# Two of eight token tiles of a PEER layer computed over all experts on TensorE, six gathered, with the fronts of later tiles run ahead

## The reference, cut to what matters

```python
q = (h @ w_q).reshape(bsz, s, PEER_HEADS, 2, PEER_HALF)
scores = jnp.einsum('bshpd,pkd->bshpk', q, sub_keys)
s_top, i_top = lax.top_k(scores, PEER_TOPK)
...
expert = i1 * PEER_N_KEYS + i2          # 8 heads x 16 picks for each token
gates = jax.nn.softmax(best, axis=-1)
act = jnp.einsum('bthkd,btd->bthk', u[eb], xb)
w = gb * jax.nn.gelu(act, approximate=False)
out = jnp.einsum('bthk,bthkd->btd', w, v[eb])
```

## Time and profile before

| | |
|---|---|
| median of three runs | 4433.24 us |
| the profiled execution: its time | 4419.49 us |
| its span, first to last instruction | 4417.6 us |
| mean granted TensorE clock | 0.735 of full |
| DVE, POOL, PE busy | 53%, 54%, 55% |
| data moved | 1201.38 MB, mean 272 GB/s |

### The profile page before, as it was taken

The page is one execution under the profiler, slowest core; times in us unless marked ns, Lnnn a source line. Parts: engine busy times, 40 slices in busy tenths (PEclk is TensorE's granted clock), DMA queues, the critical chain, the costliest instruction groups (busy, mean ns, idle before and its releaser), DMA issues.

```text
span 4417.6 us, 33711 instructions
## 1 busy us (share of the span) xinstructions
PE 2446.3 (55%) x10844; PEld 1289.7 (29%) x10844; DVE 2342.8 (53%) x4908; ACT 891.9 (20%) x2805; POOL 2404.9 (54%) x2104
## 2 busy tenths in 40 slices
PE   8999878988881543532543453354345335423333
PEld 5778756565640121210120121012012001200000
DVE  3330077674008557557546655755665675575443
ACT  1310033232021211211211221121122112111111
POOL 1333100000006777777777767777777777777775
PEclk9999989999895766755765675576578557655555
DMA  2322242120507998999989999999999999999998
GB/s 84 128 95 86 85 149 69 43 72 29 201 34 260 351 340 326 362 363 352 359 330 363 352 351 363 350 362 359 365 347 359 363 356 367 345 358 358 373 359 307
DMA packets 348199, 1201.38 MB, mean 272 GB/s; under 512 B 37248, under 2 KB 60544, under 8 KB 346384
## 3 DMA queue, kind: packets, MB, share of 16 engines
q0 software_dynamic: 294912, 1073.87, 65.6%
q1 hardware_dynamic: 53136, 125.68, 7.9%
HBM read 1166.90 MB, written 32.51 MB: 272 GB/s over the span
## 4 chain that ended last, share of the span: by engine, by line
POOL 43%; issue 13%; PE 6%; DMA 5%; DVE 2%; another core or an unknown queue 2%; ACT 0%; POOLq 0%; DVEq 0%; ACTq 0%
POOL v_ring L1295 22%; POOL u_ring L1283 21%; DMA v_ring<-in_v_dram,idx_v 4%; PE acc L1327 3%; PE small L1381 2%; DVE u_ring L1523 0%; DMA u_ring<-in_u_dram,idx 0%; PE wide L1366 0%; PE wide L1352 0%; PE wide L1391 0%; DVE work L1723 0%; DVE ihalf L1726 0%; DVE work L1718 0%; DVE idx_v L1618 0%
## 5 line engine op out<-in xcount | busy, mean ns | idle before, releaser
L1523 DVE CUSTOM_DVE_ANT_0 u_ring<-u_ring,h 128x1024 f32<-128x1024 f32 x1024 | 1250.5, 1224 | 1170.2 <-DMA u_ring<-in_u_dram,idx 1089.6
L1327 PE MATMUL acc<-v_ring,spread_w 128*32 128x512 f32 x4096 | 873.4, 988 | 1762.6 <-DMA v_ring<-in_v_dram,idx_v 1644.3
L1283 POOL DMA_INDIRECT u_ring<-in_u_dram,idx x1024 | 1091.1, 1066 | 1120.7 <-DVE idx L1728 803.5
L1295 POOL DMA_INDIRECT v_ring<-in_v_dram,idx_v x1024 | 1163.9, 1137 | 472.3 <-issue 286.8
L1327 PEld LDWEIGHTS acc<-v_ring,spread_w 128*32 128x32 f32 x4096 | 168.3, 152 | 2378.5 <-issue 2188.4
L1439 ACT ACTIVATE spread_w<-comb,w_v 128x32 f32<-128x32 f32 x1024 | 248.0, 310 | 1097.4 <-PE acc L1327 452.8
L1423 ACT ACTIVATE gelu_v<-act_u 32x4 f32<-32x4 f32 x1024 | 212.7, 208 | 980.9 <-DVE act_u L1523 689.9
L680 PE MATMUL mix_bank<-w_out,mixT 128*128 128x512 f32 x512 | 227.1, 600 | 2.4 <-ACT mixT L870 2.4
L1381 PE MATMUL small<-work,pwq 128*128 128x128 f32 x1024 | 144.6, 298 | 32.0 <-issue 30.4
L1381 PEld LDWEIGHTS small<-work,pwq 128*128 128x128 f32 x1024 | 134.1, 210 | 68.0 <-issue 66.2
L264 PE MATMUL group<-w_nat_high,x_high 128*128 128x512 f32 x384 | 150.1, 391 | 3.7 <-ACT padded L383 3.7
(11 more groups left out here) (254 smaller groups left out, 3291.1 us busy)
## 6 DMA issues: line engine op xcount, KB each, us to landing
u_ring<-in_u_dram,idx POOLq DMA_INDIRECT x1024
v_ring<-in_v_dram,idx_v POOLq DMA_INDIRECT x1024
w_nat<-in_w_nat_dram SPq DMA_DIRECT2D x6, 2048.0 KB, 8.7
nat_dram<-stage SPq DMA_DIRECT2D x48, 256.0 KB, 2.2
scanT_dram<-stage SPq DMA_DIRECT2D x22, 512.0 KB, 2.9
w_tr<-in_w_tr_dram SPq DMA_DIRECT2D x18, 512.0 KB, 4.0
gate_in<-nat_dram SPq DMA_DIRECT2D x16, 512.0 KB, 4.3
qkb<-scanT_dram SPq DMA_DIRECT2D x24, 256.0 KB, 5.2
```

Of the source, the lines that this page charges most:

```text
L1283: pool.indirect_dma_start(out=u_ring[:, g % U_RING, :], out_offset=None, in_=peer_u, in_offset=bass.IndirectOffsetOnAxis(ap=idx[:, s, n:n ...
L1295: pool.indirect_dma_start(out=v_ring[:, g % V_RING, :], out_offset=None, in_=peer_v, in_offset=bass.IndirectOffsetOnAxis(ap=idx_v[:, s, n: ...
L1327: last = pe.matmul(acc[c * QUAD:(c + 1) * QUAD, half * 512:(half + 1) * 512], spread_w[:, slot, :], v_ring[:, slot, half * 512:(half + 1) ...
L1523: dve.tensor_tensor_reduce(out=row, in0=row, in1=h2[:, s, :], scale=1.0, scalar=0.0, op0=ALU.mult, op1=ALU.add, accum_out=act_u[:, (n // T ...
```

## The change

Tiles 0 to 5 are gathered as before, in 768 slots. Tiles 6 and 7 (256 tokens, DT) are computed over all 16384 experts on PE. For that:

- Fronts are packed: 58 stages into 24 slots, then 40 chunks into 32 slots, one front after the other from slot 39 to slot 430. Their results wait in five buffers of idx, idx_v and gates_v; h2 goes to DRAM and is read back for its tile (`store_h2`, `load_h2`). For tiles 6 and 7 the picks stay as two key numbers and a gate per pick.
- At slot 433 PE transposes h2 and the picks of tiles 6 and 7 (`turn_dense`).
- 288 ticks are spread over slots 433 to 751. In each half of the first keys (b), 16 ticks build the gate of each of 64 x 128 experts for 256 tokens: DVE writes one-hot rows for 8 tokens at a time (`hots`), PE multiplies them (`choose`), ACT copies the result into the tables' space (`keep_chosen`). Then 128 ticks run 64 blocks of 128 experts: `dense_u` (8 products of 256 columns), `dense_gelu`, `dense_weigh`, `dense_v` (4 products of 512 columns).
- SP streams uT (u, transposed on the host) and v, 512 KB for each block and each of the two, into rings of three.
- The norms of tiles 6 and 7 are at slots 754 to 761; their stores and that of tile 5 come last.

The diff, cut to its core:

```diff
+FRONT_STAGES = 58
+STAGE_SLOTS = 24
+CHUNK_SLOTS = 32
+GATHERED = 6
+DENSE = TILES - GATHERED
+DT = DENSE * P
+KEPT = 5
+HALF_KEYS = NKEYS // 2
+TOKENS = 8
+GROUPS = DT // TOKENS
+GROUP_TICKS = GROUPS // 2
+HALF_TICKS = GROUP_TICKS + 2 * HALF_KEYS
+STREAM = 3
...
+        idx_v = sb("idx_v", [P, KEPT, PICKS], mybir.dt.int32)
+        gates_v = sb("gates_v", [P, KEPT, PICKS], F32)
+        idx = sb("idx", [P, KEPT, PICKS], mybir.dt.int32)
...
+        chosen = tables[:, :, :, :].rearrange("p a k n -> p (a k n)").rearrange("p (i t) -> p i t", t=DT)
+        dense_h2 = tables[:, 1, KC - DENSE:KC, :]
+        stream = pwq[:, :, :].rearrange("p k n -> p (k n)")
+        uT_ring = stream[:, 0:STREAM * D].rearrange("p (s k e) -> p s k e", s=STREAM, k=KC)
+        vb_ring = stream[:, STREAM * D:2 * STREAM * D].rearrange("p (s n) -> p s n", s=STREAM)
+        dense_hT = stream[:, 2 * STREAM * D:2 * STREAM * D + KC * DT].rearrange("p (k t) -> p k t", k=KC)
+        hot2 = work[:, 0:2 * D].rearrange("p (s t i) -> p s t i", s=2, t=TOKENS)
...
+        gelu_d = work[:, 3 * D:3 * D + 2 * DT].rearrange("p (s t) -> p s t", s=2)
...
+        picksT = h1[:, 0:3 * DT].rearrange("p (w t) -> p w t", w=3)
...
+        SPAN = STAGE_SLOTS + CHUNK_SLOTS
+        SLOTS = GATHERED * PICKS
+        DENSE_AT = FIRST_LATE + (TILES - 1) * SPAN + 2
+        DENSE_END = SLOTS - 16
...
-            for t in range(TILES):
-                body(t, t % 2, t < TILES - 1)
-            last(TILES, 0)
...
+            for t in range(GATHERED):
+                body(t, t % 2)
+            last(GATHERED, 0)
...
+            return FIRST_LATE + (f - 1) * SPAN
+        def stages_at(slot):
+            f = (slot - FIRST_LATE) // SPAN + 1
...
+            at = slot - begins(f)
+            return f, [n for n in range(FRONT_STAGES) if n * STAGE_SLOTS // FRONT_STAGES == at]
+        def chunks_at(slot):
...
+            at = slot - begins(f) - STAGE_SLOTS
+            return f, [c for c in range(CHUNKS) if c * CHUNK_SLOTS // CHUNKS == at]
+        def ticks_at(slot):
+            span = DENSE_END - DENSE_AT
+            first, last = (-(-(slot + d - DENSE_AT) * 2 * HALF_TICKS // span) for d in (0, 1))
+            return range(first, last) if DENSE_AT <= slot < DENSE_END else range(0)
...
+            return DENSE_AT + tick * (DENSE_END - DENSE_AT) // (2 * HALF_TICKS)
+        def block_tick(i, late):
+            b, j = i // HALF_KEYS, i % HALF_KEYS
+            return b * HALF_TICKS + GROUP_TICKS + (j if j < 2 else 2 * j - 2) + late
...
+                def store_h2(f):
+                    sp.wait_ge(h2_ready, f + 1)
+                    sp.dma_start(h2_dram[f], pre2).then_inc(h2_stored, 16)
+                def load_h2(t):
+                    sp.wait_ge(h2_stored, 16 * t)
+                    if t >= 2:
+                        sp.wait_ge(y3_stored, 16 * (t - 1))
+                    sp.dma_start(h2[:, t % 2, :], h2_dram[t]).then_inc(h2_loaded, 16)
...
+                def load_uT(i):
+                    if i == 0:
+                        sp.wait_ge(pq_made, TILES)
+                    if i >= STREAM:
+                        sp.wait_ge(uT_used, i - STREAM + 1)
+                    sp.dma_start(uT_ring[:, i % STREAM, :, :], peer_uT[i]).then_inc(uT_landed[i % STREAM], 16)
+                def load_vb(i):
...
+                        sp.wait_ge(vb_used, i - STREAM + 1)
+                    sp.dma_start(vb_ring[:, i % STREAM, :], peer_v[i * NKEYS:(i + 1) * NKEYS, :]
+                                 ).then_inc(vb_landed[i % STREAM], 16)
...
+                for slot in range(SLOTS):
+                    f, stages = stages_at(slot)
+                    if 38 in stages:
+                        store_h2(f)
+                        if f < TILES - 1:
+                            next_h1(f + 1)
+                        if f == 1:
+                            load_h2(1)
+                        if f == TILES - 1:
+                            load_dense_h2()
+                    t, n = slot // PICKS - 1, slot % PICKS
+                    if t >= 0 and n == LAG + 8:
+                        store_y3(t, t + 1, h2[:, t % 2, :])
+                        if t + 2 < GATHERED:
+                            load_h2(t + 2)
+                    if slot == begins(TILES - 1) + STAGE_SLOTS:
+                        for i in range(STREAM):
+                            load_uT(i)
+                            load_vb(i)
+                    for i in range(STREAM, NKEYS):
+                        if tick_slot(block_tick(i - STREAM, 1)) == slot:
+                            load_uT(i)
+                        if tick_slot(block_tick(i - STREAM, 5)) == slot:
+                            load_vb(i)
+                    if slot == tick_slot(HALF_TICKS + GROUP_TICKS + 8):
...
+                def turn_dense():
+                    pe.wait_ge(dense_loaded, 16)
+                    pe.wait_ge(keyscores_ready, TILES)
+                    for e, to in enumerate((small[:, :], wide[:, 0:D])):
+                        for k in range(KC):
+                            last = pe.transpose(to[:, k * P:(k + 1) * P], dense_h2[:, e, k * P:(k + 1) * P], ident[:, :])
+                    last.then_inc(dense_turned, 1)
+                    pe.wait_ge(picks_ready, DENSE)
+                    for w, kind in enumerate((idx_v, gates_v, idx)):
+                        for e in range(DENSE):
+                            at = D + w * DT + e * P
+                            last = pe.transpose(wide[:, at:at + P], kind[:, (GATHERED + e) % KEPT, :].bitcast(F32),
...
+                def choose(b, q):
+                    turn = b * GROUPS + q
+                    pe.wait_ge(hot_ready, turn + 1)
+                    if turn < 2:
+                        pe.wait_ge(dense_ready, 1)
+                    elif q < 2:
+                        pe.wait_ge(gelu_d_done, HALF_KEYS)
+                    else:
+                        pe.wait_ge(chosen_ready, turn - 1)
+                    for j in range(TOKENS):
+                        at = q % 2 * 512 + j * HALF_KEYS
+                        last = pe.matmul(small[:, at:at + HALF_KEYS], hot2[:, q % 2, j, :], hot1[:, q % 2, j, :],
+                                         start=True, stop=True)
+                    last.then_inc(chosen_made, 1)
+                def dense_u(i):
+                    pe.wait_ge(uT_landed[i % STREAM], 16 * (i // STREAM + 1))
+                    if i % HALF_KEYS < 2:
+                        pe.wait_ge(chosen_ready, GROUPS * (i // HALF_KEYS + 1))
+                    else:
+                        pe.wait_ge(gelu_d_done, i - 1)
+                    at = i % 2 * 512
+                    for k in range(KC):
+                        last = pe.matmul(small[:, at:at + DT], uT_ring[:, i % STREAM, k, :], dense_hT[:, k, :],
+                                         start=(k == 0), stop=(k == KC - 1))
+                    last.then_inc(uT_used, 1)
+                def dense_v(i):
+                    pe.wait_ge(vb_landed[i % STREAM], 16 * (i // STREAM + 1))
+                    pe.wait_ge(wT_ready, i + 1)
...
+                    for e in range(DENSE):
+                        for c in range(2):
+                            at = e * D + c * 512
+                            last = pe.matmul(wide[:, at:at + 512], chosen[:, i % HALF_KEYS, e * P:(e + 1) * P],
+                                             vb_ring[:, i % STREAM, c * 512:(c + 1) * 512],
+                                             start=(i == 0), stop=(i == NKEYS - 1))
+                    last.then_inc(vb_used, 1)
+                def dense(tick):
+                    b, r = tick // HALF_TICKS, tick % HALF_TICKS
+                    if r < GROUP_TICKS:
+                        for q in (2 * r, 2 * r + 1):
+                            choose(b, q)
+                    at, base = r - GROUP_TICKS, b * HALF_KEYS
+                    if at in (0, 1):
+                        dense_u(base + at)
+                    elif at in (2 * HALF_KEYS - 2, 2 * HALF_KEYS - 1):
+                        dense_v(base + at - HALF_KEYS)
+                    elif at >= 2 and at % 2 == 0:
+                        dense_u(base + at // 2 + 1)
+                    elif at >= 3:
+                        dense_v(base + (at - 3) // 2)
...
+                def turned_dense():
...
+                    for e, source in enumerate((small[:, :], wide[:, 0:D])):
+                        last = act.activation(dense_hT[:, :, e * P:(e + 1) * P],
+                                              source.rearrange("p (k t) -> p k t", k=KC), ACT.Copy)
...
+                    act.activation(picksT, wide[:, D:D + 3 * DT].rearrange("p (w t) -> p w t", w=3),
+                                   ACT.Copy).then_inc(picksT_ready, 1)
+                def keep_chosen(b, q):
+                    act.wait_ge(chosen_made, b * GROUPS + q + 1)
+                    if b == 1 and q == 0:
+                        act.wait_ge(vb_used, HALF_KEYS)
```

(59 more changed lines are left out.)

227 lines of the change are left out of this document (141 added, 86 removed).

## The result

The changed kernel has a median of 4163.89 us over four runs (4156.74 to 4167.89), where the kernel before, run beside it, had 4432.66 (4403.42 to 4433.83): a ratio of 0.9407 (interval 0.9365 to 0.9448), 6% faster. Forecast were 4363 us, in a range of 4180 to 4560.

A forecast was written before the change was run, and what follows sets the result against it. DMA bytes were taken as the bound, the kernel running 4% above that floor. First dot 1353.8, slots to 39 89.4, fronts 1330, dense 1482, slots 752–767 44, tail 48.3: 4347.5; plus 1.9 and 13.8, 4363 us; range 4180 to 4560.

The forecast's parts named there:

- the floor of DMA in the products: Products, per block: 2.215 slots at 2.83 us plus 2.91 for streams, 9.18 us; with today's 4% 9.6, taken as 9.7.
- the lower bound of 9.2: Products: least time forecast for one block, 9.2 us, where 9.7 was taken and 11.2 was the upper bound.
- The sign of the change: Whole kernel: claimed to end 70 us earlier than now; chance of faster 0.61, same 0.08, slower 0.31.
- PE in the products: Products, per block: dense_u 3.47, dense_v 3.45 and combines 1.06 us, 7.98 us of PE at the full clock.
- The fronts: Slots 39 to 431: seven fronts of 56 slots, period 190 us each, 1330 us; bounds 1204 and 1484.
- The ring: Each front: stages (97 us, bounds 84 and 108), then picks (93 us), without overlapping the next front.
- the picks: Second part of each front, 32 slots: set by DVE's work, 93 us; bounds 88 and 104.
- Choosing: Dense part, two stretches building the gates: 112 us each, 224 in all; bounds 100 and 144 each.
- The turn: Slots 431 to 433: two slots (6 us), then transposes and copies (10 us), 16 us.
- First dot, end and tail: Start and finish: first dot at 1353.8 us, slots 752 to 767 44 us, tail 48.3 us.
- Rival 1: Fronts stay hidden: 56 slots take 165 us, 175 less in all, 4188 us; chance 0.13.
- Rival 2: Products: PE falls to the lower clock level, 11.2 us a block, 192 more, 4555 us; chance 0.19.
- Rival 3: Picks: POOL becomes the bound, 107 us in place of 93, 98 more, 4461 us; chance 0.13.

## Why the prediction was wrong, and where it was right

**The step that failed** is the floor of DMA in the products: "DMA: 2.215 x 2.83 + 2.91 = 9.18 us", and with it "with the 4% of today 9.6 ... I take 9.7" and the lower bound of 9.2. I took the share of the gathers' queue, 65.6% for 1073.87 MB, for time that the engines must spend, and a sum of two queues for their common cost. But time per packet isn't a property of the packet: gathers alone contain long ones, and with the engines full they do not. What paced the gathers of the kernel before was POOL's issuing, as far as the traces tell: its groups, which I had read as waiting "mostly for its own issue", show 9.9 us of waits for a buffer in 350. So 2.83 us was not a floor of DMA. At 410 GB/s a slot costs 2.56 and a block's streams 2.56, and 2.215 x 2.56 + 2.56 is 8.23 us, not 9.18. Measured are 410 GB/s with two queues (373 with one on the same chip, 349 to 365 in the kernel before), and 64 blocks of 3.371 MB in 529.5 us are 407, so a block costs 3.371 / 0.409 = 8.24 us. The sum with the measured 8.27: 4347.5 - 128 x (9.7 - 8.27) = 4164.5 in the span, against 4158.3. The sign of the change was right, as it hung on bytes removed; its size was 70 us of 269.

The Trainium skill ("DMA: Bandwidth & Descriptors", Where 436 GB/s comes from) lets the HBM side bind transfers from HBM at about 358 GB/s and gives 435 for the engines' ports. The rate of the gathers in the kernel before, 349 beside a front and 365 without, looks like the first; 409 in this kernel and 410 in two experiments lie above it and 6% below the second. So the measurement decides against the lower limit here, with one core at work.

**PE in the products** was right: 7.98 us forecast, 8.01 measured where v wasn't streamed. With 32 and 40 stage slots the same sum gives 7.80 and 7.61 us, and 7.78 and 7.55 were measured. That PE stands close behind DMA was said; that it stands within 3% was missed, because DMA's 9.18 was wrong.

**The fronts** were right in sum by luck, through two errors that cancel. The ring from the h1T copy to the end of the score copy took 90 us on average over the seven fronts (85.0 to 93.7; forecast 97, bounds 84 and 108), the picks 94.3 (92.0 to 98.7; forecast 93), and then 3 to 9 us passed until the next front's copy, which I had left out of the ring. DVE's picks start at once when ACT's copy of the scores ends, as in these lines of the changed kernel's timeline, ACT's and then DVE's:

```profile
1721.38 1.94 ACT L1676 ACTIVATE work<-wide 128x1024 f32<-128x1024 f32 x2 [3.41 <-PE wide L1515]
...
1723.35 1.64 DVE L1899 MAX8 vals<-work 128x8 f32<-128x128 f32 x8 [14.85 <-ACT work L1676]
```

The chain of the same stages (start, length, what) shows the combines inside it that the forecast priced at 1.92 to 3.64 us, among the products:

```profile
1661.15 12.21 PE wide L1490 x28
1673.37 1.85 PE acc L1451 x16
1675.22 2.28 PE wide L1490 x4
...
1688.02 3.35 PE acc L1451 x16
1691.37 5.52 PE small L1505 x47
```

What the forecast took from front 0, PE's work and copies in a row, doesn't set a stage stretch by itself: with 87 us of it gone the seven fronts were 14 us shorter. PE's waits for gathered rows grew in its place; what keeps those rows late isn't shown.

**Choosing** was right, 113.6 and 115.0 for 112 each; 512 columns on DVE measured 689 ns (forecast 0.69 us) and 1024 took 1219. **The turn** is right in its parts but in the wrong row: two slots passed in 2.3 us, as the rows of the rings had landed, and its transposes and copies lie in the first choosing stretch. I counted the slots at the pace of gathers, 13.7 us too much. First dot, end and tail were right within 8 us.

**Rival 1** (fronts hidden, 4188) lies near the measured time and did not happen: a period was 191 us, not 165. **Rival 2** (PE at the lower level) did not happen in the products: granted clock 0.99, busy 98%. DMA's shorter block pushed PE's share up from the 0.83 that I had reckoned. The Trainium skill ("TensorE: Matmul & The Clock Gate", HAM oscillation) warns of waits between bursts; PE waited 9.2 us in 529 at the combines and the clock stood at 0.99, so the rule had little to work on. In the choosing PE waited 14.2 us in 115 with a clock of 0.62, but without the gates' product it waited 12.6 in 102 and had 0.71. Whether such short waits throw the clock back isn't shown. **Rival 3** (POOL) did not come at its price, 107 us for the picks, but its sign did. In the picks of tile 2's front, 1723 to 1818 us, POOL had no time to spare:

```profile
L1407 POOL DMA_INDIRECT u_ring<-in_u_dram,idx x30 | 37.6, 1254 | 9.1 <-issue 9.1
L1419 POOL DMA_INDIRECT v_ring<-in_v_dram,idx_v x30 | 35.6, 1185 | 11.8 <-issue 8.5 <-remote 1.7 <-PE acc L1451 1.6
```

Its 60 gathers took 1.22 us each (0.94 undisturbed) and 0.30 before each, 91 of 94 us, with one wait of 1.6 us for a buffer. DVE was busy 88 of the same 94. The forecast's 93 us for DVE's work came true, yet POOL was as full beside it, and which of the two would hold the picks without the other isn't shown.

**What stays open.** Gathers alone ran at 373 GB/s on two chips, at 365 in the kernel before on a third. POOL sets that pace by the traces, but why its instructions take 1.06 us on average where an undisturbed one takes 0.94, and what an idle engine has to do with the long packets, isn't shown. Nor is why the fronts took 1339, 1264 and 1307 us on three chips while the products took 529 to 530 per half on each. The gain is 6%, 2.4% and 5.7% there, mostly because the kernel before took 4433, 4197 and 4393 us; that its gathers make this difference is likely, but it was traced on one chip only.

## What to carry to other kernels

A queue's share of busy time is what its packets took, not what they need: before a stream is added beside gathers, take the floor from the highest rate in GB/s that any stretch or a small experiment with two queues shows, not from share per byte, and look whether the engine that issues the gathers ever waits for a free buffer. If it doesn't, it sets the pace and not DMA, and bytes added from another queue cost less than the share says. When work moves beside other work, write both bounds per unit (here 8.24 us of DMA and 7.98 of PE a block), as the larger one sets the time and the smaller one how much can still be won. A change of layout such as the number of slots for a front must be run on one chip beside its base, since chips differed here by more than the effect.

## What the runs showed of the hardware that I had not expected

- Two queues together moved 408 to 410 GB/s on every chip, one of gathers alone 373 with a share of 0.98, where POOL issued without a pause; the share of the sum reads 1.01 to 1.03, so it isn't capped at 1.
- The same kernel took 4193 to 4433 us on different chips, 5.7% apart. Of the changed kernel the gathers beside fronts differ (1264 to 1339 us), products and choosing hardly do.
- PE busy for 89% of a stretch had a granted clock of 0.62 in the choosing, and for 88% one of 0.92 in the kernel before. The busy share alone doesn't tell the clock. In the choosing PE stopped for DVE in group after group and ran short products; which of these keeps the clock low isn't shown.
- Half the columns were no cheaper: a record of 64 columns took 0.181 us in the choosing (89.6 us for 496) at 0.62; one of 128 took 0.125 in front 0 of the kernel before at 0.90, which at 0.62 would by estimate be 0.18. Each of them has its own weight load, and PEld was busy 90 of the 115 us of the choosing.
